# The last portion of the first modulation: from row products on TensorE to scaling on ScalarE and adding on GpSimd

## The chip, the cores and the metric

One core of one Trainium2 chip. The metric is the device time of one execution in microseconds (us); of several runs the median is compared.

## The reference, cut to what matters

The kernel computes one layer of a decoder for 256 tokens of width 1024. The change touches how the first modulation, a vector of 2 x 1024 numbers (shift and scale), comes out of the conditioning vector c:

```python
c_act = jax.nn.silu(c)                                  # c: (1, 1024)
mod = c_act @ w_ada[l] + b_ada[l]                       # w_ada: (1024, 6 * 1024)
sh1, sc1, g1, sh2, sc2, g2 = [m[:, None, :] for m in jnp.split(mod, 6, axis=-1)]
h = rms_norm(x, g_pre_mix[l]) * (1.0 + sc1) + sh1       # (1, 256, 1024)
y = hybrid_mixer(h, w_in[l], ...)                       # starts with h @ w_in
...
```

Everything is float32. Only sh1 and sc1, and of them only the last 256 of 1024 channels, are computed in another way after the change.

## The kernel before, in words

The kernel writes every engine's instructions out by hand, with semaphores between engines. The 1024 channels of h are KC = 8 chunks of 128, which lie on the partitions. The first ten output units (FIRST_UNIT = 10) of h @ w_in are computed chunk by chunk: for chunk k TensorE multiplies the chunk's columns of w_in by chunk k of h, and adds into eight PSUM banks. Each product takes three passes, since an operand is split into a rounded high part and the rest: ScalarE copies the raw weights into the high part (`chunk_cut_hi`, L862, or L886 for a whole chunk of 128x1224) and makes the high part of h (`chunk_h_hi`, L868); VectorE subtracts to get the low parts (L1243, L1289 and L1276). A chunk is 30 matmuls of 128x256 (all on L1641).

Chunk k of h can't be made before its shift and scale are there. These come in three portions, PORTION = [0, 3, 6, 8]: channels of chunks 0 to 2, 3 to 5, and 6 and 7. For each portion SyncE loads the columns of w_ada into the tile `ada`, four pairs of rows with a semaphore each (`load_ada`, L539). The tile holds for partition p the eight rows p*8 to p*8+7 of w_ada, so that `ada[:, k, a, :]` times `csil[:, k]` (silu(c), laid out in the same way) summed over k and over the partitions is the result. `row_products` (L1595) does that on TensorE: the weights are silu(c) repeated 32 times (`crep`), and `ada` streams past them, eight matmuls for two pairs, each in two records of the profile. ScalarE copies the row from PSUM to SBUF (`keep_row`, L856), TensorE turns it into columns (`turn_first` L1606, `turn_others` L1612), and VectorE adds bias and gain to give the columns `col` (`first_columns` L1250, `other_columns` L1259).

Where the row products stand in TensorE's order is a table: PRODUCTS_AT maps (chunk, number of matmuls of it that are done) to pairs, TURN_ROW_AT to the turn. Portion 2's products stand behind matmul 15 of chunk 4 and behind matmul 7 of chunk 5, its turn behind matmul 19 of chunk 5. Chunk 6 needs the columns. GpSimd builds masks in the first 4 us and has nothing to do from then until it loads further columns of w_ada for the second modulation (`load_part`, L672), once chunk 7 of h is made. `acc` is a tile of 128x2048 that holds squares of x at the start and those further sums later.

```python
            PRODUCTS_AT = {(1, 28): ((1, 0), (1, 1)), (2, 13): ((1, 2),), (2, 17): ((1, 3),), (4, 15): ((2, 0), (2, 1)), (5, 7): ((2, 2), (2, 3))}
            TURN_ROW_AT = {(2, 26): 1, (5, 19): 2}
```

Of the kernel before, what the change touches and what calls it, by code (L numbers as in the profile page):

```python
# [19 lines left out]
F32 = mybir.dt.float32  # L20
F32R = mybir.dt.float32r
ALU = mybir.AluOpType
ACT = mybir.ActivationFunctionType
AX_X = mybir.AxisListType.X

P = 128
D = 1024
KC = D // P
# [51 lines left out]
PORTION = [0, 3, 6, KC]  # L80
N_PORTIONS = len(PORTION) - 1
ADA_COLS = 3 * P
# [6 lines left out]
def columns_made(k):  # L89

    g = portion_of(k)
    return 4 * g + (2 if k == PORTION[g] else 4)
# [182 lines left out]
def decoder_layer(nc, x, c, w_ada, b_ada, g_pre_mix, g_post_mix, w_in, b_gate, w_proj_sb,  # L275
                  w_proj_moba, w_proj_dsa, w_o, g_pre_ffn, g_post_ffn, w_up, w_down, out):
    ctx = ExitStack()
    with ctx:
# [3 lines left out]
        def sem(name):  # L282
            return ctx.enter_context(nc.semaphore(name))
# [16 lines left out]
        csil = csil_all[:, 0:KC]  # L300
# [10 lines left out]
        ones = sb("ones", [P, P], F32R)  # L311
# [9 lines left out]
        acc = sb("acc", [P, 2 * D], scope=mix)  # L321
# [35 lines left out]
        gated_part.close()  # L357


        cut_part = ExitStack()  # L360
        sb("cut_pad", [P, TT * D + (3 * KC + N_OCH + FULL_OCH) * S + 2 * D + BANK + 4 * CAUSAL + 4 * P + 2 * TT * 8 + VEC_END],
           scope=cut_part)
# [3 lines left out]
        start = ExitStack()  # L366
        ada = sb("ada", [P, KC, 2, ADA_COLS], scope=start)
# [15 lines left out]
        bank = [psum[:, i, :] for i in range(8)]  # L383
# [5 lines left out]
        ada_in, mod_first, mod_cols = [sem(f"ada_in{p}") for p in range(KC // 2)], sem("mod_first"), sem("mod_cols")  # L389
# [2 lines left out]
        x_kept_act, x_kept_dve = sem("x_kept_act"), sem("x_kept_dve")  # L392
        x_raw_turned, root_ready, root_turned, rootrow_ready = (sem("x_raw_turned"), sem("root_ready"), sem("root_turned"),
                                                                sem("rootrow_ready"))
        row_kept, mod_turned, x_scaled, tmp_ready, chunk_hi, chunk_lo, chunk_done = (
            sem("row_kept"), sem("mod_turned"), sem("x_scaled"), sem("tmp_ready"), sem("chunk_hi"), sem("chunk_lo"), sem("chunk_done"))
        wo_in = [sem(f"wo_in{k}") for k in range(KC)]
# [14 lines left out]
        ss_ready, var_ready, sqrt_ready, xn_ready = sem("ss_ready"), sem("var_ready"), sem("sqrt_ready"), sem("xn_ready")  # L412
# [3 lines left out]
        ones_set, gate_in, gate_bias_in, gate_done, gate_hi, gate_lo, gate_ready = (  # L416
            sem("ones_set"), sem("gate_in"), sem("gate_bias_in"), sem("gate_done"), sem("gate_hi"), sem("gate_lo"), sem("gate_ready"))
# [7 lines left out]
        ln_ready, sp_ready, sp_masked, sp_hi, sp_lo, sums, a_ready, a_masked = (sem("ln_ready"), sem("sp_ready"), sem("sp_masked"), sem("sp_hi"), sem("sp_lo"),  # L425
                                                                 sem("sums"), sem("a_ready"), sem("a_masked"))
# [219 lines left out]
        def _(pool):  # L646
# [16 lines left out]
            def load_part(n):  # L663

                g, k, a = ADA_PARTS[n]
                if n < 2:
                    pool.wait_ge(tmp_ready, KC)
                    pool.wait_ge(chunk_hi, KC)
                else:
                    pool.wait_ge(acc_done, n - 1)  # L670
                c0 = D * (2 * g + a)
                pool.dma_start(ada_part[n % 2], ada_dram[:, k, c0:c0 + D]).then_inc(part_in[n % 2], 16)  # L672
# [6 lines left out]
            def load_gain(g):  # L679

                pool.wait_ge(gain_out[g], 16)
                pool.dma_start(gb[g][:, :], gain_dram[g:g + 1, :].to_broadcast([P, D])).then_inc(gain_in[g], 16)

            load_part(0)
            load_part(1)
            for u in range(FIRST_UNIT, N_UNITS):
# [6 lines left out]
                if u in SECOND_AT and SECOND_AT[u] in SB_NO:  # L693

                    i = SB_NO[SECOND_AT[u]]
                    n = SECOND_AT[u]
# [4 lines left out]
                if u in EXP_AT and EXP_AT[u] in SB_NO:  # L701

                    n = EXP_AT[u]
# [27 lines left out]
        def _(act):  # L731
# [102 lines left out]
            for w, k0 in ((b_ada, VEC_ADA), (g_pre_mix, VEC_PRE_MIX), (b_gate, VEC_GATE),  # L834
                          (g_post_mix, VEC_POST_MIX), (g_pre_ffn, VEC_PRE_FFN), (g_post_ffn, VEC_POST_FFN)):
                n = w.shape[0] * w.shape[1] // P
# [14 lines left out]
            def keep_row(g, c0, c1):  # L851

                act.wait_ge(gemv, (KC // 2) * (g + 1))
                if g:
                    act.wait_ge(mod_turned, g)
                act.activation(mrow[:, P * c0:P * c1], bank[5][:, P * c0:P * c1], ACT.Copy).then_inc(row_kept, 1)  # L856
# [7 lines left out]
            def chunk_h_hi(k):  # L864
# [3 lines left out]
                act.activation(hhi[:, k, :], h32[:, k, :], ACT.Identity, bias=col[0][:, k:k + 1],  # L868
                               scale=col[0][:, KC + k:KC + k + 1]).then_inc(chunk_hi, 1)

            for k in range(KC):
                if k in PORTION:
                    g = portion_of(k)
                    n = PORTION[g + 1] - k
                    keep_row(g, 0, 1)
                    if g:
                        keep_row(g, 1, n)
                    chunk_cut_hi(k, True)
                    chunk_h_hi(k)
                    chunk_cut_hi(k, False)  # L880
                    if g == 0:
                        keep_row(g, 1, n)
                else:
                    act.wait_ge(front_in[k], 16)
                    act.wait_ge(back_in[k], 16)
                    act.activation(chunk_view(whi, end_hi, k), chunk_view(raw, None, k), ACT.Copy).then_inc(w_hi, 2)  # L886
                    chunk_h_hi(k)
                if k == 2:
                    act.wait_ge(consts, 2)
                    act.activation(ones[:, :], neg1[:, :], ACT.Copy, scale=-1.0).then_inc(ones_set, 1)  # L890
                    act.activation(neg_all[:, :], neg1[:, :], ACT.Copy).then_inc(ones_set, 1)
                if k == KC - 1:
                    act.preload_act_table_set("natural_log_exp_and_others")
            for q in range(4):
# [4 lines left out]
            for u in range(FIRST_UNIT, N_UNITS):  # L899
# [4 lines left out]
                if u in EXP_AT and EXP_AT[u] in SB_NO:  # L904
                    n = EXP_AT[u]
# [12 lines left out]
                if u in NORM_AT and NORM_AT[u] in SB_NO:  # L918
                    n = NORM_AT[u]
# [9 lines left out]
                if u in EXP_AT and EXP_AT[u] in SOFT_NO:  # L929

                    n = EXP_AT[u]
# [8 lines left out]
                    for t, (c0, c1) in enumerate(((0, P), (P, CAUSAL))):  # L940
                        ins = act.activation(bufp[n % 2][:, c0:c1], bufa[n % 2][:, c0:c1], ACT.Exp,
                                             scale=SLOPES[2 * h + (branch == "ds")],
# [7 lines left out]
                if u in SECOND_AT:  # L950
                    n = SECOND_AT[u]
# [624 lines left out]
        def _(pe):  # L1576
# [31 lines left out]
            def turn_others(g):  # L1608

                pe.wait_ge(row_kept, 2 * g + 2)  # L1610
                for c in range(1, PORTION[g + 1] - PORTION[g]):
                    mm = pe.matmul(bank[6][:, 2 * c - 2:2 * c], mrow[:, P * c:P * (c + 1)], pick[:, :], start=True, stop=True)  # L1612
                mm.then_inc(mod_turned, 1)


            PRODUCTS_AT = {(1, 28): ((1, 0), (1, 1)), (2, 13): ((1, 2),), (2, 17): ((1, 3),), (4, 15): ((2, 0), (2, 1)), (5, 7): ((2, 2), (2, 3))}
            TURN_ROW_AT = {(2, 26): 1, (5, 19): 2}

            def warm_up(n):

# [159 lines left out]
            for t in range(TT):  # L1780
                mm = pe.transpose(bank[3][:, S + P * t:S + P * (t + 1)], rinv[:, t:t + 1].to_broadcast([P, P]), ident[:, :])
# [42 lines left out]
            def modulation_between(k, n):  # L1824

                for g, p in PRODUCTS_AT.get((k, n), ()):
                    row_products(g, p)
                if (k, n) in TURN_ROW_AT:
                    turn_first(TURN_ROW_AT[k, n])
                    turn_others(TURN_ROW_AT[k, n])  # L1830

            for k in range(KC - 1):
                if k in PORTION:
# [4 lines left out]
                for n, (i, u) in enumerate((i, u) for i in (0, 2, 1) for u in range(FIRST_UNIT)):  # L1838
# [4 lines left out]
                    mm = first_unit(u, k, (i,))  # L1843
# [4 lines left out]
            k = KC - 1  # L1848
# [37 lines left out]
            for f in range(KC):  # L1886
# [10 lines left out]
                for i, branch in enumerate(("sb", "mb", "ds")):  # L1897
                    dst = branches(f)[:, S * i:S * (i + 1)]
                    for c, ch in enumerate(BRANCH_CHUNKS[branch]):
                        if ch < FULL_OCH:  # L1900
                            mm = three(dst, [x[:, ch, :] for x in w], [ohi[:, ch, :], olo[:, ch, :]], c == 0, c == 2)
# [174 lines left out]
```

## Time and profile before

| what | value |
|---|---|
| median of 3 runs | 455.38 us (455.24 to 456.07) |
| profiled execution, time | 456.04 us |
| profiled execution, span | 454.3 us |
| busy share PE, DVE, ACT, POOL | 97%, 73%, 54%, 8% |
| share of PE in the chain that ended last | 94% |
| mean granted TensorE clock | 0.997 of full speed |

The span is that of one profiled execution, from its first to its last instruction; the time beside it is what the same execution took as a whole, 1.7 us more. PE is TensorE's matmuls, DVE is VectorE, ACT ScalarE, POOL GpSimd and SP SyncE; an L with a number is a line of the kernel, and times in the trace are in us from the start of the span.

### The profile page before, as it was taken

What the parts mean: (1) busy time and instruction counts of PE and PEld (TensorE: products, weight loads), DVE (VectorE), ACT (ScalarE), POOL (GpSimd) and SP (SyncE); (2) the same over time, 40 slices, a digit from 0 to 9 for tenths busy, and PEclk for the clock granted to TensorE, in tenths of its full rate; (3) what the DMA queues carried; (4) which work ended last, traced back from release to release, by engine and by line L of the source; (5) the groups of instructions that cost most, each with busy time, mean ns of one, the idle gap of its engine ahead of it and who ended that gap; (6) DMA issues with size and microseconds to landing.
All of it is one profiled execution on the core that took longest, in us unless ns stands there. A gap on an engine that the chain in (4) does not pass through costs nothing.

```text
span 454.3 us, 7880 instructions
## 1 busy us (share of the span) xinstructions
PE 439.9 (97%) x2966; PEld 388.9 (86%) x2966; DVE 330.7 (73%) x587; ACT 243.7 (54%) x432; POOL 34.8 (8%) x76
## 2 busy tenths in 40 slices
PE   4999999999999999999999999999999999999994
PEld 3678988999999899989997899888888888888883
DVE  4625668787998887956995785796696687678655
ACT  4424884556777656596553686533534525425332
POOL 2000102000322231000000001000000000000000
PEclk9999999999999999999999999999999999999998
DMA  8999466886788658746659526988648657530002
GB/s 288 383 378 345 153 231 222 280 297 236 241 302 291 188 180 283 235 150 202 195 200 365 186 68 184 378 302 277 228 159 269 218 190 272 185 138 0 1 0 92
DMA packets 61634, 99.86 MB, mean 220 GB/s; under 512 B 3892, under 2 KB 44452, under 8 KB 61604
## 3 DMA queue, kind: packets, MB, share of 16 engines
q1 hardware_dynamic: 56480, 81.57, 53.2%
q0 software_dynamic: 4960, 17.84, 11.5%
q8 instruction: 19, 0.31, 0.3%
q14 instruction: 11, 0.09, 0.1%
q10 hardware_dynamic: 164, 0.05, 0.0%
HBM read 98.40 MB, written 1.05 MB: 219 GB/s over the span
## 4 chain that ended last, share of the span: by engine, by line
PE 94%; DVE 2%; DMA 1%; issue 1%; ACT 1%; SPq 0%; DVEq 0%; ACTq 0%
PE psum L1579 17%; PE psum L1994 16%; PE psum L1580 16%; PE psum L1581 16%; PE psum L1995 8%; PE psum L1641 7%; PE psum L1941 3%; PE psum L1595 2%; PE psum L1768 1%; DVE wlo L1113 1%; DMA xt<-in_x_dram 1%; PE psum L1703 1%; PE psum L1701 1%; PE psum L1630 1%; PE psum L1750 1%
## 5 line engine op out<-in xcount | busy, mean ns | idle before, releaser
L1994 PE MATMUL psum<-hcut,whi 128*128 128x512 f32 x320 | 111.7, 392 | 0.0
L1995 PE MATMUL psum<-hcut,wlo 128*128 128x256 f32 x320 | 89.6, 280 | 0.0
L1579 PE MATMUL psum<-hcut,whi 128*128 128x256 f32 x280 | 82.1, 293 | 0.3 <-DVE wlo L1113 0.3
L1580 PE MATMUL psum<-hcut,whi 128*128 128x256 f32 x280 | 79.1, 283 | 0.0
L1581 PE MATMUL psum<-hcut,wlo 128*128 128x256 f32 x280 | 79.1, 282 | 0.0
L1113 DVE TENSOR_TENSOR wlo<-raw,whi 128x768 fp32r<-128x768 f32 (+3 forms) x68 | 64.4, 973 | 15.3 <-ACT whi L749 14.7
L1994 PEld LDWEIGHTS psum<-hcut,whi 128*128 128x128 f32 x320 | 59.9, 187 | 13.3
L1995 PEld LDWEIGHTS psum<-hcut,wlo 128*128 128x128 f32 x320 | 60.5, 189 | 0.3
L749 ACT ACTIVATE whi<-raw 128x768 fp32r<-128x768 f32 (+3 forms) x68 | 55.6, 850 | 6.8 <-PE psum L1905 3.2
L1579 PEld LDWEIGHTS psum<-hcut,whi 128*128 128x128 f32 x280 | 53.4, 191 | 5.5 <-ACT qk L829 2.0
L1580 PEld LDWEIGHTS psum<-hcut,whi 128*128 128x128 f32 x280 | 53.5, 191 | 0.0
L1581 PEld LDWEIGHTS psum<-hcut,wlo 128*128 128x128 f32 x280 | 53.5, 191 | 0.0
L1490 DVE TENSOR_TENSOR dlo<-draw,dhi 128x2048 fp32r<-128x2048 f32 x11 | 25.1, 2292 | 35.6 <-ACT dhi L1008 35.6
L1485 DVE TENSOR_TENSOR wlo<-raw,whi 128x1024 fp32r<-128x1024 f32 x36 | 42.4, 1220 | 3.0 <-ACT whi L1001 3.0
L1057 ACT ACTIVATE fsil<-fsil 128x256 f32<-128x256 f32 x20 | 8.4, 418 | 63.5 <-DVE fsil L1504 63.5
L1001 ACT ACTIVATE whi<-raw 128x1024 fp32r<-128x1024 f32 x36 | 35.9, 1045 | 0.0
L1580 PE MATMUL psum<-dlo,fhi 128*128 128x512 f32 x88 | 34.4, 391 | 0.0
L1579 PE MATMUL psum<-dhi,fhi 128*128 128x512 f32 x88 | 34.4, 391 | 0.0
L1581 PE MATMUL psum<-dhi,flo 128*128 128x512 f32 x88 | 34.2, 389 | 0.0
L1008 ACT ACTIVATE dhi<-draw 128x2048 fp32r<-128x2048 f32 x11 | 21.0, 1915 | 22.5 <-PE psum L1581 22.5
L1184 DVE SCALAR_TENSOR_TENSOR acc<-xn,csil,acc 128x1024 f32<-128x1024 f32 x21 | 26.9, 1282 | 4.6 <-DMA xn<-in_w_ada_dram 4.1
L1580 PE MATMUL psum<-wlo,hcut 128*128 128x320 f32 (+2 forms) x76 | 26.2, 345 | 0.0
(252 smaller groups left out, 817.3 us busy)
## 6 DMA issues: line engine op xcount, KB each, us to landing
raw<-in_w_up_dram SPq DMA_DIRECT2D x22, 1024.0 KB, 7.6
xn<-in_w_ada_dram POOLq DMA_DIRECT2D x32, 512.0 KB, 4.9
raw<-in_w_in_dram SPq DMA_DIRECT2D x6, 2048.0 KB, 9.0
draw<-in_w_down_dram SPq DMA_DIRECT2D x11, 1024.0 KB, 5.0
ada<-in_w_ada_dram SPq DMA_DIRECT2D x16, 384.0 KB, 9.2
raw<-in_w_in_dram SPq DMA_DIRECT2D x3, 1536.0 KB, 8.9
raw<-in_w_o_dram SPq DMA_DIRECT2D x8, 512.0 KB, 4.6
raw<-in_w_in_dram SPq DMA_DIRECT2D x3, 1280.0 KB, 7.0
```

The source lines that it names most:

```text
L749: act.activation(block_view(whi[b % 2], b)[0:p, chunks, cols], block_view(raw[b % 2], b)[0:p, chunks, cols], ACT.Copy).then_inc(w_hi, 1)
L1001: act.activation(block_view(whi[part], B_FFN)[:, 2 * q:2 * q + 2, :], block_view(raw[part], B_FFN)[:, 2 * q:2 * q + 2, :], ACT.Copy).then_ ...
L1113: dve.tensor_tensor(block_view(wlo[b % 2], b)[0:p, chunks, cols], block_view(raw[b % 2], b)[0:p, chunks, cols], block_view(whi[b % 2], b)[ ...
L1184: ins = dve.scalar_tensor_tensor(sums, part, csil[:, k:k + 1], sums, ALU.mult, ALU.add)
L1485: dve.tensor_tensor(block_view(wlo[part], B_FFN)[:, 2 * q:2 * q + 2, :], block_view(raw[part], B_FFN)[:, 2 * q:2 * q + 2, :], block_view(w ...
L1490: dve.tensor_tensor(dlo[slot][:, :, :], draw[slot][:, :, :], dhi[slot][:, :, :].bitcast(F32), ALU.subtract).then_inc(d_lo, 1)
L1579: pe.matmul(dst, a[0], b[0], start=first, stop=False)
L1580: pe.matmul(dst, a[0], b[1], start=False, stop=False)
L1581: return pe.matmul(dst, a[1], b[0], start=False, stop=last)
L1641: mm = pe.matmul(first_place(u)[0:n, :], w, h[:, k, :], start=k == 0 and i == 0 and u in (1, 2, 4, 6, 8), stop=k == KC - 1 and i == 2, ski ...
L1994: pe.matmul(dst[:, :], wh, hcut[:, k, :, :].rearrange("p a s -> p (a s)"), start=k == 0, stop=False)
L1995: mm = pe.matmul(dst[:, S:2 * S], wl, hhi[:, k, :], start=False, stop=k == KC - 1)
```

## The change

Portions 0 and 1 stay as they are. For portion 2, ScalarE multiplies `ada[:, k, :, 0:256]` in place by `csil[:, k]` for k = 0 to 7 (`scale_last`), two pairs behind chunk 4 and two behind chunk 5 (LAST_PAIRS_AT). GpSimd adds the eight up, into a part of `acc`: seven adds of 128x512, each waiting for the scaled operand and for the add before. TensorE then sums over the partitions with four matmuls (`last_columns`), whose weights are 128 columns of the sums and which stream one column of ones; they give columns at once, so the row copies and the turn are gone. They stand behind matmul 17 of chunk 5.

```diff
--- before.py
+++ after.py
@@ -357,6 +357,9 @@
         gated_part.close()
 
 
+        last_sums = acc[:, 0:2 * ADA_COLS].rearrange("p (a n) -> p a n", a=2)
+
+
         cut_part = ExitStack()
         sb("cut_pad", [P, TT * D + (3 * KC + N_OCH + FULL_OCH) * S + 2 * D + BANK + 4 * CAUSAL + 4 * P + 2 * TT * 8 + VEC_END],
            scope=cut_part)
@@ -392,6 +395,7 @@
         x_kept_act, x_kept_dve = sem("x_kept_act"), sem("x_kept_dve")
         x_raw_turned, root_ready, root_turned, rootrow_ready = (sem("x_raw_turned"), sem("root_ready"), sem("root_turned"),
                                                                 sem("rootrow_ready"))
+        last_scaled, last_added = sem("last_scaled"), sem("last_added")
         row_kept, mod_turned, x_scaled, tmp_ready, chunk_hi, chunk_lo, chunk_done = (
             sem("row_kept"), sem("mod_turned"), sem("x_scaled"), sem("tmp_ready"), sem("chunk_hi"), sem("chunk_lo"), sem("chunk_done"))
         wo_in = [sem(f"wo_in{k}") for k in range(KC)]
@@ -681,6 +685,17 @@
                 pool.wait_ge(gain_out[g], 16)
                 pool.dma_start(gb[g][:, :], gain_dram[g:g + 1, :].to_broadcast([P, D])).then_inc(gain_in[g], 16)
 
+
+            n_last = P * (PORTION[-1] - PORTION[-2])
+            sums = last_sums[:, :, 0:n_last]
+            for k in range(1, KC):
+                pool.wait_ge(last_scaled, k + 1)
+                if k == 1:
+                    pool.wait_ge(ss_ready, 4)
+                else:
+                    pool.wait_ge(last_added, k - 1)
+                pool.tensor_tensor(sums, ada[:, 0, :, 0:n_last] if k == 1 else sums, ada[:, k, :, 0:n_last], ALU.add).then_inc(last_added, 1)
+
             load_part(0)
             load_part(1)
             for u in range(FIRST_UNIT, N_UNITS):
@@ -868,12 +883,23 @@
                 act.activation(hhi[:, k, :], h32[:, k, :], ACT.Identity, bias=col[0][:, k:k + 1],
                                scale=col[0][:, KC + k:KC + k + 1]).then_inc(chunk_hi, 1)
 
+            def scale_last(p):
+
+                act.wait_ge(ada_in[p], 32 * N_PORTIONS)
+                for k in (2 * p, 2 * p + 1):
+                    part = ada[:, k, :, 0:P * (PORTION[-1] - PORTION[-2])]
+                    act.activation(part, part, ACT.Copy, scale=csil[:, k:k + 1]).then_inc(last_scaled, 1)
+
+
+            LAST_PAIRS_AT = {4: (0, 1), 5: (2, 3)}
+
             for k in range(KC):
                 if k in PORTION:
                     g = portion_of(k)
                     n = PORTION[g + 1] - k
-                    keep_row(g, 0, 1)
-                    if g:
+                    if g < N_PORTIONS - 1:
+                        keep_row(g, 0, 1)
+                    if 0 < g < N_PORTIONS - 1:
                         keep_row(g, 1, n)
                     chunk_cut_hi(k, True)
                     chunk_h_hi(k)
@@ -889,6 +915,8 @@
                     act.wait_ge(consts, 2)
                     act.activation(ones[:, :], neg1[:, :], ACT.Copy, scale=-1.0).then_inc(ones_set, 1)
                     act.activation(neg_all[:, :], neg1[:, :], ACT.Copy).then_inc(ones_set, 1)
+                for p in LAST_PAIRS_AT.get(k, ()):
+                    scale_last(p)
                 if k == KC - 1:
                     act.preload_act_table_set("natural_log_exp_and_others")
             for q in range(4):
@@ -1613,8 +1641,22 @@
                 mm.then_inc(mod_turned, 1)
 
 
-            PRODUCTS_AT = {(1, 28): ((1, 0), (1, 1)), (2, 13): ((1, 2),), (2, 17): ((1, 3),), (4, 15): ((2, 0), (2, 1)), (5, 7): ((2, 2), (2, 3))}
-            TURN_ROW_AT = {(2, 26): 1, (5, 19): 2}
+            PRODUCTS_AT = {(1, 28): ((1, 0), (1, 1)), (2, 13): ((1, 2),), (2, 17): ((1, 3),)}
+            TURN_ROW_AT = {(2, 26): 1}
+            LAST_COLUMNS_AT = (5, 17)
+
+            def last_columns():
+
+                pe.wait_ge(last_added, KC - 1)
+                pe.wait_ge(ones_set, 1)
+                pe.wait_ge(mod_cols, columns_made(PORTION[-2] - 1))
+                for c in range(PORTION[-1] - PORTION[-2]):
+                    for a in range(2):
+                        dst = bank[6][:, 2 * c - 2 + a:2 * c - 1 + a] if c else bank[7][:, a:a + 1]
+                        mm = pe.matmul(dst, last_sums[:, a, P * c:P * (c + 1)], ones[:, 0:1].bitcast(F32), start=True, stop=True)
+                    if c == 0:
+                        mm.then_inc(mod_first, 1)
+                mm.then_inc(mod_turned, 1)
 
             def warm_up(n):
 
@@ -1828,6 +1870,8 @@
                 if (k, n) in TURN_ROW_AT:
                     turn_first(TURN_ROW_AT[k, n])
                     turn_others(TURN_ROW_AT[k, n])
+                if (k, n) == LAST_COLUMNS_AT:
+                    last_columns()
 
             for k in range(KC - 1):
                 if k in PORTION:
```

In TensorE's order, around chunks 4 and 5 of the first ten units (hcut is h, whi and wlo the high and low parts of w_in), before:

```order
L1641 MATMUL psum<-hcut,wlo 128x256 x4
L1595 MATMUL psum<-ada,crep 32x256 x8
L1641 MATMUL psum<-hcut,wlo 128x256 x5
L1641 MATMUL psum<-hcut,whi 72x256
L1641 MATMUL psum<-hcut,whi 128x256 x9
L1641 MATMUL psum<-hcut,whi 72x256
L1641 MATMUL psum<-hcut,whi 128x256 x6
L1595 MATMUL psum<-ada,crep 32x256 x8
L1641 MATMUL psum<-hcut,whi 128x256 x3
L1641 MATMUL psum<-hcut,wlo 72x256
L1641 MATMUL psum<-hcut,wlo 128x256 x8
L1606 MATMUL psum<-pick,mrow 128x2
```

and after the change, up to the beginning of chunk 6:

```order
L1683 MATMUL psum<-hcut,wlo 128x256 x9
L1683 MATMUL psum<-hcut,whi 72x256
L1683 MATMUL psum<-hcut,whi 128x256 x9
L1683 MATMUL psum<-hcut,whi 72x256
L1683 MATMUL psum<-hcut,whi 128x256 x9
L1683 MATMUL psum<-hcut,wlo 72x256
L1683 MATMUL psum<-hcut,wlo 128x256 x6
L1656 MATMUL psum<-ones,acc 128x1 x4
L1683 MATMUL psum<-hcut,wlo 128x256 x3
L1683 MATMUL psum<-hcut,whi 72x256
L1683 MATMUL psum<-hcut,whi 128x256 x9
L1683 MATMUL psum<-hcut,end_hi 128x256
```

The sixteen row products are gone, and four matmuls of one column stand where the two turning ones stood, two places earlier.

In ScalarE's order, after the change, from chunk 4's cut to chunk 6's:

```order
L912 ACTIVATE whi<-raw 128x1224
L883 ACTIVATE hcut<-xn,col 128x256
L891 ACTIVATE ada<-ada,csil 128x2x256 x4
L912 ACTIVATE whi<-raw 128x1224
L883 ACTIVATE hcut<-xn,col 128x256
L891 ACTIVATE ada<-ada,csil 128x2x256 x4
L877 ACTIVATE end_hi<-raw 128x584
```

Before, the two L891 rows weren't there, and two copies `mrow<-psum 128x128` stood where the second one stands now: the first four scalings are now ahead of chunk 5's cut.

In GpSimd's order, after the change, from the masks to the first load:

```order
L664 AFFINE_SELECT dist<-dist 128x128 x2
L697 TENSOR_TENSOR acc<-ada 128x2x256
L697 TENSOR_TENSOR acc<-acc,ada 128x2x256 x6
L676 DMA xn<-in_w_ada_dram 128x1024 x3
```

The seven adds stand in what was one long wait.

## Rows read from the trace of the kernel before

**Rows 1.** The page, part 1: busy time, share of the span, instructions
```profile
PE 439.9 (97%) x2966; PEld 388.9 (86%) x2966; DVE 330.7 (73%) x587; ACT 243.7 (54%) x432; POOL 34.8 (8%) x76
```

**Rows 2.** Chain of waits, 30 to 56 us: start us, us, what
```profile
39.83 1.00 PE psum L1595 x16
...
43.63 1.00 PE psum L1595 x16
...
46.24 0.12 PE psum L1606 x2
46.35 0.22 PE psum L1612 x2
46.58 8.73 PE psum L1641 x71
```

**Rows 3.** Timeline of PE, start of chunk 6: start us, us, instruction
```profile
47.83 1.35 PE L1641 MATMUL psum<-hcut,end_hi 128*128 128x256 f32 x10
```

**Rows 4.** What waited on PE, whole span: us in total, times, longest us
```profile
PE psum L1579 <- DVE wlo L1113: 0.3, 1, 0.3
```

**Rows 5.** Timeline of ACT, 34 to 50 us
```profile
36.08 0.60 ACT L868 ACTIVATE hcut<-xn,col 128x256 fp32r<-128x256 f32 x1 [0.18 <-DVE col L1261]
36.59 1.22 ACT L886 ACTIVATE whi<-raw 128x1224 fp32r<-128x1224 f32 x1
37.71 0.58 ACT L868 ACTIVATE hcut<-xn,col 128x256 fp32r<-128x256 f32 x1
44.70 0.45 ACT L856 ACTIVATE mrow<-psum 128x128 f32<-128x128 f32 x2 [6.40 <-PE psum L1595]
```

**Rows 6.** Loads of ada, line L539, first pair of portion 2
```profile
L539 SPq DMA_DIRECT2D ada<-in_w_ada_dram x2: 378/448/517, 27.0 to 27.4; - x2
DMA to landing us min/median/max: 6.7/7.3/8.0
```

**Rows 7.** The same, its last pair
```profile
L539 SPq DMA_DIRECT2D ada<-in_w_ada_dram x2: 368/686/1003, 31.8 to 32.2; - x2
DMA to landing us min/median/max: 6.4/7.0/7.6
```

**Rows 8.** Groups by form, ACT: busy us, mean ns
```profile
L1033 ACT ACTIVATE xn<-xt,rinv 128x512 f32<-128x512 f32 x2 | 1.4, 715 | 0.8 <-DVEq L1137 0.8
```

**Rows 9.** Groups by form, POOL
```profile
L657 POOL CAST dist<-bufa 128x384 f32<-128x384 int32 x1 | 0.5, 502 | 0.0
...
L2064 POOL MEMSET const-float32-1.0<- 128x1 f32 x1 | 0.1, 98 | 0.0
```

**Rows 10.** Timeline of DVE, 36 to 50 us
```profile
38.42 1.43 DVE L1289 TENSOR_TENSOR wlo<-raw,whi 128x1224 fp32r<-128x1224 f32 x1
39.76 0.42 DVE L1276 TENSOR_TENSOR hcut<-bufp,hcut 128x256 fp32r<-128x256 f32 x1
```

**Rows 11.** Timeline of POOL, 0 to 62 us, and then 120 to 124 us
```profile
3.12 0.54 POOL L660 TENSOR_SCALAR_AFFINE_SELECT dist<-dist 128x128 f32<-128x128 f32 x2
...
120.55 2.50 POOL L707 TENSOR_SCALAR_AFFINE_SELECT bufp<-bufp 128x128 f32<-128x128 f32 x2 [2.10 <-DVE bufp L1357]
```

**Rows 12.** Timeline of DVE, 120 to 124 us
```profile
120.39 1.28 DVE L1184 SCALAR_TENSOR_TENSOR acc<-xn,csil,acc 128x1024 f32<-128x1024 f32 x1
121.58 2.54 DVE L1113 TENSOR_TENSOR wlo<-raw,whi 128x1024 fp32r<-128x1024 f32 x2
```

**Rows 13.** Windows at the end: stretch and length, busy by engine, PEclk, DMA
```profile
447.00:449.00 2.00, 1.17 (x6) 0.63 (x4) 0.75 (x2) 1.22 (x4) 0.00 (x0) 1.00 0.52 193
449.00:451.00 2.00, 0.00 (x0) 0.00 (x0) 1.89 (x6) 0.29 (x2) 0.00 (x0) 1.00 0.00 0
451.00:452.00 1.00, 0.00 (x0) 0.00 (x0) 0.84 (x2) 0.00 (x0) 0.00 (x0) 0.69 0.00 0
```

**Rows 14.** Chain of waits, first 13 us
```profile
9.92 1.35 PE psum L1595 x8
...
12.29 0.78 PE psum L1595 x8
```

## Prediction

> **What bounds the kernel now.** I read the busy shares first: TensorE is busy 97% of the span, GpSimd 8% [rows 1]. Then the chain of waits: from 30 to 56 us it is TensorE without a gap worth naming, and in it stand the two blocks of portion 2's row products, 1.00 us each, and the turn, 0.12 + 0.22 us [rows 2]. Then the list of waits: behind the start-up TensorE waits for another engine once, 0.3 us for VectorE near 124 us [rows 4]. So a microsecond that TensorE loses or wins between 40 and 50 us is lost or won in the total, but for some 0.3 us. The timelines of ScalarE and VectorE show what room they have there: ScalarE finishes chunk 5 of h at 38.3 us and then waits 6.40 us for the row of portion 2 [rows 5]; VectorE finishes chunk 5 at 40.2 us [rows 10]. GpSimd's masks end at 3.7 us [rows 11], and it has no work until 50 us.
>
> **TensorE, what goes and what comes.** Removed: 2 x 1.00 us of products and the turn, 0.12 + 0.22 = 0.34 us [rows 2]. Added: four matmuls with 128x128 float32 weights and one streamed column. The nearest rows are the two turning matmuls with the same weights and two columns, 0.34 us for the two [rows 2]; I take 0.8 us for four, with 0.68 as the low end and 0.9 as the high one (0.22 each for all). Net: 2.34 - 0.8 = **1.5 us less** if TensorE doesn't wait.
>
> **When TensorE comes to the new place.** Before, the turn stood behind matmul 19 of chunk 5 at 46.24 us [rows 2]. Without the products (-2.00) and two matmuls earlier (-0.25, from chunk 6's ten in 1.35 us with 0.12 from one to the next [rows 3]) TensorE is there at 44.0 us. If the sums are ready at time T, later than 44.0, the rest follows: 0.8 us for the columns and 13 matmuls of 0.114 us, 1.5 us (11 of them took 46.58 to 47.83 before [rows 2, 3]), and chunk 6 starts at T + 2.3. Before it started at 47.83. So **the change costs T - 45.5 us**, and T = 44.0 gives back the -1.5 above. Chunk 6 of h is not later than that: its first column needs half of the four matmuls (0.4), then VectorE and ScalarE as before, about 1.1 us, together T + 1.5.
>
> **ScalarE.** A scaling is 128x512 with a factor per partition; the same form took 0.715 us [rows 8], 0.62 from start to start when several follow (the cut of 1.22 us at 36.59 and the next at 37.71 show the 0.1 overlap [rows 5]). Its operands are there: the first pair of portion 2 lands at 27.4 + 8.0 = 35.4 us [rows 6], the last at 32.2 + 7.6 = 39.8 us [rows 7]. So four scalings run from 36.6 to 39.1, chunk 5's cut to 40.3, chunk 5 of h to 40.8, and four more from 40.7 to 43.3 us. Chunk 5 on TensorE starts near 41.5 (1.00 us earlier than before by the first products [rows 2]), so the delay of 2.5 us that chunk 5's cut gets has 0.7 us to spare. VectorE's subtraction for it moves from 38.4 to 40.3, ends 1.43 us later at 41.7 [rows 10], and its first use is ten matmuls behind 41.5, at 42.6. These parts cost nothing; that cover is thin, and half a microsecond more on ScalarE would show, but would be swallowed by the wait that comes next. The two row copies that go (0.45 us [rows 5]) free ScalarE where it was idle.
>
> **GpSimd, the term that decides.** The trace has no addition on GpSimd. Its nearest row with a streamed input is a cast of 128x384, 0.502 us; an instruction of one element takes 0.098 us [rows 9]. So one stream costs 0.404 us for 384 elements, 0.54 for 512. Low end for an add: one stream and the fixed part, 0.64 us. High end: the whole cast scaled up and doubled, 1.34 us. An add reads two tensors, and I take the streams one after the other: 0.10 + 2 x 0.54 = 1.17 us, and 0.1 us for the wait on its own semaphore, 1.27 from add to add. The Trainium skill, GPSIMD Engine Reference, section Performance versus the Vector engine, gives 4497 ns for a float32 add of 2048 elements; an estimate from that page is 1.1 to 1.2 us for 512, which would give the same sum within 0.3 us, where the single stream would give a kernel that is faster.
>
> The first add can start when two operands are scaled, at 38.0 us. Seven in a chain take 8.9 us: 46.9 us. The later operands (the last at 43.3) are never what an add waits for at this rate.
>
> On top comes VectorE. Two mask instructions of GpSimd took 2.50 us at 120.55, while VectorE ran a 1.28 us instruction with two tensor inputs and then subtractions of 1.2 us, where two of the same shape took 0.54 us on an idle chip [rows 11, 12]: each was held up for one VectorE instruction. In the adds' way stand chunk 5's subtraction, 1.43 us, and the 0.42 us one behind it [rows 10]. I count the large one, 1.4 us, with 0 and 1.85 as ends. The Trainium skill, SBUF — State Buffer, states that a VectorE instruction with two SBUF inputs and a GpSimd one that reads SBUF exclude each other for a whole instruction; by that page the full 1.4 stands, and the trace agrees in those rows.
>
> T = 38.0 + 8.9 + 1.4 = **48.3 us**: TensorE waits 4.3 us, and the cost is 48.3 - 45.5 = **+2.8 us**. Behind it all of VectorE's and ScalarE's work for chunks 6 and 7, and the load that waits for chunk 7's cut, moves with T; TensorE has 0.7 us more between T and chunk 6 than it had between the turn and chunk 6 (2.3 against 1.6), so none of them becomes a new wait. GpSimd's queue holds its first loads for the second modulation behind the adds; they wait for chunk 7 of h anyway, so the adds cost them nothing.
>
> The profiled execution took 456.04 us, 0.66 over the median of 455.38. I add to the median: 455.38 + 2.8 = 458.2 us. (In a profile: 456.04 + 2.8 = 458.8, a span of 457.1.)
>
> **The rivals.** *A, the forecast*: the adds take about 1.2 us each, blocked or not. Unblocked T is 46.9 and the cost +1.4, at the high ends +4; its own range is 456.7 to 459.4. For it speaks that an add has two streams and the cast one. Chance 0.48.
>
> *B, the clock falls*: TensorE would stand idle 4.3 us. At the end of the span its last matmul ends at 448.2, and the granted clock is 1.00 until 451 and 0.69 in the mean of the next microsecond [rows 13], so it fell from the 2.4 GHz level to that of 1.2 about 3.2 us behind the last matmul. At the start, eight products took 1.35 us, later 0.78 [rows 14], 1.7 times as long, and the slow ones came although TensorE had worked since 5 us. If the clock falls in the wait and 3 to 6 us of work run slowly, 1.3 to 2.6 us are added: 459.5 to 460.8. The Trainium skill, TensorE: Matmul & The Clock Gate, states the same of long idle gaps in the middle of a kernel. Against it: one drop in the trace says when it came once, not that every wait of 4 us brings it, and T may be earlier. Chance 0.22.
>
> *C, faster*: GpSimd streams both tensors at once, 0.64 + 0.1 us an add. Then ScalarE sets the end: its last product at 43.3, one add behind it, T = 44.1 and -1.4 us: 454.0. It decides from T under 44.6, which is an add-to-add time under 0.9 us if nothing blocks. For it: the mask instructions, which also read and write, are quick alone (0.27 us). Chance 0.14.
>
> *D, no difference*: an add-to-add time of 0.95 to 1.1 us without blocking, T 44.7 to 46.0, between -0.8 and +0.5: 454.6 to 455.9. Also the case in which VectorE's and TensorE's gains cancel. Chance 0.16.
>
> **How the numbers follow.** A measurement of this kernel can tell about 0.2%, 0.9 us, from no change. C is faster, with a little of D: 0.15. D without that, and A's lowest edge: 0.17. The rest of A and B: 0.68. The range reaches down to 454.2, which leaves out half of C, and up to 460.8, which leaves out the worst of B and of the price of an add: about 0.15 outside.
>
> **What would show it.** In the profile after: seven adds on GpSimd with 1.2 to 1.3 us from start to start and one gap or long one of some 1.4 us beside VectorE's 128x1224 subtraction; TensorE's four one-column matmuls starting near 48 us with a wait of 4 us for GpSimd ahead of them; chunk 6 near 50.6; scalings of 0.7 us on ScalarE with the last ending near 43.3. I am wrong if the adds come every 0.9 us or faster, if TensorE waits at chunk 5's start for ScalarE for more than a few tenths, or if what is lost at 48 us isn't in the total. A granted clock below 1.00 between 46 and 55 us would show B.

## The result, and the profile after

The changed kernel takes **461.3 us** in the median (460.59 to 462.72, 6 runs), the kernel before 455.44 us (455.13 to 456.27, 6 runs). The ratio is 1.0126, with a 95% interval of 1.0114 to 1.0137: 5.7 us slower. The forecast was 458.2 (+2.8 us) with a range of 454.2 to 460.8: the right side, half the size, and the measured time is outside the range. The profiled execution of the changed kernel took 460.59 us, with a span of 458.9.

The page of the kernel after, parts 1 and 2 (busy time; the granted clock in tenths by 40 slices of 11.5 us):

```profile
PE 439.4 (96%) x2938; PEld 390.6 (85%) x2938; DVE 333.4 (73%) x587; ACT 248.2 (54%) x438; POOL 44.2 (10%) x83
...
PEclk9999799999999999999999999999999999999998
```

Against [rows 1], TensorE has 28 instructions fewer and hardly less busy time, and GpSimd is busy 9.4 us more. New is the 7 in the fifth slice, 46 to 57 us. The wait that is new in that kernel's list of what TensorE waited for (us in total, times, longest; before: [rows 4]):

```profile
PE psum L1656 <- POOL acc L697: 5.3, 1, 5.3
```

The timeline of its POOL, 34 to 62 us, and a part of its chain of waits, 36 to 60 us (the chain now runs through GpSimd):

```profile
37.24 1.33 POOL L697 TENSOR_TENSOR acc<-ada 128x512 f32<-128x512 f32 x1 [33.58 <-ACT ada L891]
38.72 9.35 POOL L697 TENSOR_TENSOR acc<-acc,ada 128x512 f32<-128x512 f32 x6
```

```profile
40.16 2.31 POOL acc L697
...
42.60 1.27 POOL acc L697
...
46.81 1.27 POOL acc L697
...
48.13 1.86 PE psum L1656 x8
```

An add takes 1.27 us and the next starts 1.40 us after it; one took 2.31. The seventh ends at 48.08. The timelines of its ACT and DVE in the same place:

```profile
35.84 2.56 ACT L891 ACTIVATE ada<-ada,csil 128x512 f32<-128x512 f32 x4
38.31 1.21 ACT L912 ACTIVATE whi<-raw 128x1224 fp32r<-128x1224 f32 x1
39.43 0.58 ACT L883 ACTIVATE hcut<-xn,col 128x256 fp32r<-128x256 f32 x1
39.91 2.55 ACT L891 ACTIVATE ada<-ada,csil 128x512 f32<-128x512 f32 x4
```

```profile
37.34 1.39 DVE L1297 TENSOR_SCALAR bufp<-xn,col 128x256 f32<-128x256 f32 x1
39.62 1.68 DVE L1317 TENSOR_TENSOR wlo<-raw,whi 128x1224 fp32r<-128x1224 f32 x1 [0.90 <-ACT whi L912]
41.23 1.52 DVE L1304 TENSOR_TENSOR hcut<-bufp,hcut 128x256 fp32r<-128x256 f32 x1
```

ScalarE does what was forecast: four scalings in 2.56 us, the last ending at 42.46. This execution is 0.75 us ahead of the one before already at chunk 4 of h (35.33 against 36.08 in [rows 5]), so times of the two are compared after adding that; most of what follows is compared by lengths instead of by times. On VectorE, instructions of 0.4 us take 1.4 and 1.5 while GpSimd adds. Its PE, 38 to 62 us, and the windows around the wait (length, busy time of PE, PEld, DVE, ACT, POOL, granted clock, DMA share, GB/s):

```profile
41.84 0.98 PE L1683 MATMUL psum<-hcut,wlo 128*72 128x256 f32 x7
48.13 1.86 PE L1656 MATMUL psum<-ones,acc 128*128 128x1 f32 x8 [5.31 <-POOL acc L697]
49.85 0.99 PE L1683 MATMUL psum<-hcut,wlo 128*128 128x256 f32 x3
50.64 2.33 PE L1683 MATMUL psum<-hcut,whi 128*72 128x256 f32 x10
52.77 1.73 PE L1683 MATMUL psum<-hcut,end_hi 128*128 128x256 f32 x10
```

```profile
44.00:46.00 2.00, 0.00 (x0) 0.00 (x0) 0.00 (x0) 0.00 (x0) 1.85 (x2) 1.00 0.46 162
46.00:48.00 2.00, 0.00 (x0) 0.00 (x0) 0.00 (x0) 0.00 (x0) 1.86 (x2) 0.69 0.02 6
48.00:50.00 2.00, 1.87 (x9) 1.87 (x10) 0.79 (x4) 0.45 (x1) 0.07 (x1) 0.50 0.00 0
50.00:52.00 2.00, 2.00 (x10) 2.00 (x11) 1.97 (x6) 1.90 (x3) 0.00 (x0) 0.50 0.00 0
52.00:54.00 2.00, 2.00 (x13) 2.00 (x13) 1.96 (x4) 1.89 (x3) 0.68 (x1) 0.60 0.00 0
```

TensorE stands from 42.8 to 48.1 us with nothing to do. Within the wait the granted clock falls to 0.50, the level of 1.2 GHz, and is back at 2.4 GHz near 53.6: the eight records of the one-column matmuls take 1.86 us, ten matmuls of chunk 5 take 2.33 where ten took 1.35 in [rows 3]. From the end of the adds to chunk 6 it is 4.7 us, where 2.3 was forecast.

Where the 5.7 us arise can be read without the start-up: from the start of ScalarE's copy for chunk 4 of h (36.08 before, 35.33 after) to TensorE's first matmul behind the first ten units. That matmul is, before and after:

```profile
55.34 0.41 PE L1579 MATMUL psum<-whi,hcut 128*128 128x320 f32 x1
```

```profile
60.27 0.31 PE L1607 MATMUL psum<-whi,hcut 128*128 128x320 f32 x1
```

The stretch is 19.26 us long before and 24.94 after, 5.7 more. So what the change loses is lost there. The experiments below are read with the same stretch, each in its one profiled execution.

### The profile page after: what moved, and what is told of

It reads as the page before. It is cut to its first block, busy times and chain, and to the rows that moved or that the text cites. A ratio compares the mean times of both kernels' runs of the same rounds, so it can differ in the third digit from the quotient of the medians.

```text
span 458.9 us, 7842 instructions
## 1 busy us (share of the span) xinstructions
PE 439.4 (96%) x2938; PEld 390.6 (85%) x2938; DVE 333.4 (73%) x587; ACT 248.2 (54%) x438; POOL 44.2 (10%) x83
## 4 chain that ended last, share of the span: by engine, by line
PE 89%; DVE 3%; POOL 2%; DMA 2%; issue 1%; SPq 1%; ACT 1%; DVEq 0%; POOLq 0%; ACTq 0%
PE psum L1607 17%; PE psum L2038 16%; PE psum L1608 16%; PE psum L1609 16%; PE psum L2039 8%; PE psum L1683 5%; PE psum L1985 3%; POOL acc L697 2%; DMA ada<-in_w_ada_dram 2%; PE psum L1810 1%; DVE wlo L1141 1%; PE psum L1745 1%; PE psum L1743 1%; PE psum L1623 1%; SPq L543 1%
```

## The experiments

Two questions: how the 5.7 us divide between the wait and the clock, and whether GpSimd or ScalarE cost anything else on the way. Theory 1: a wait for seven slow adds, and a fallen clock on top. Its rivals differ by experiment. Ratios are to the kernel before in runs on the same chip, with their 95% interval; 1% is 4.56 us.

**The wait filled with transposes.** In `last_columns`, ahead of the wait:

```diff
+                for _ in range(40):
+                    pe.transpose(bank[5][:, 0:P], ident[:, :], ident[:, :])
```

> The changed kernel with 40 transposes of 128x128 into a PSUM bank that nobody reads, ahead of TensorE's wait for the sums: 40 x 0.125 = 5.0 us of work in a wait of 5.3 us. Theory 1 (the change costs a wait and, on top, a fallen clock): the granted clock stays at 1.00, the sums are ready at the same time (7 adds of 1.27 to 1.3 us, one of them held up), and the cost against the kernel before falls from 5.9 to about 3.2 us, ratio 1.007. Rival (all of the 5.9 us is the wait and what is late behind it; the clock costs nothing): 5.9 us, ratio 1.013.

Measured: ratio 1.0069 (1.0053 to 1.0085), +3.1 us, median 459.31. The mean granted clock was 0.997 or 0.998 in five of seven executions and 0.994 in two, where the changed kernel had 0.987 to 0.990 in all six of its own (the kernel before has 0.996 to 0.998; its clock falls only at the end of its span [rows 13]). The profiled execution is one of the two: a short fall, after the transposes. It is also the slowest of the seven, 462.66 us, but 2 us of that are start-up: its copy for chunk 4 of h starts at 38.13 us. The rival's 5.9 us is out: the clock costs 1.0126 - 1.0069, 2.6 us, and the wait alone 3.1. By the two intervals such a difference is uncertain by some 0.9 us.

**The same with ordinary matmuls.**

```diff
+                for _ in range(40):
+                    pe.matmul(bank[5][:, 0:S], whi[0][:, 0:P], hhi[:, 0, :], start=True, stop=True)
```

> As e1_busy_wait, with 40 matmuls of 128x256 of the kernel's usual type in place of the 40 transposes, 40 x 0.118 = 4.7 us. With transposes the mean granted clock was 0.997 in five executions and 0.994 in two. Theory 1: the clock stays, in all or nearly all executions, cost that of the wait alone, +3.1 to +3.5 us, ratio 1.007 to 1.008. If only uninterrupted work counted, the 0.6 us of wait that is left would still bring a fall in some: up to +5 us in those.

Measured: 1.0082 (1.0069 to 1.0095), +3.7 us, and a clock of 0.996 to 0.998 in all five executions. PE in its profile:

```profile
43.48 4.96 PE L1651 MATMUL psum<-hcut,whi 128*128 128x256 f32 x40
49.05 1.05 PE L1658 MATMUL psum<-ones,acc 128*128 128x1 f32 x8 [0.61 <-POOL acc L697]
...
51.58 1.36 PE L1685 MATMUL psum<-hcut,end_hi 128*128 128x256 f32 x10
```

At full clock the four column matmuls take 0.9 us (49.05 to 49.96, where the next starts), and chunk 6 starts 2.5 us after their start, where the forecast had 2.3. The wait costs 3.1 to 3.7 us, the clock 2.0 to 2.6. The traces divide it in the same way: the stretch from chunk 4 of h to the end of the first ten units takes 22.59 us here (36.13 to 58.72), 3.3 more than before, and 24.94 in the changed kernel, so the clock has 2.35 us of the 5.7.

**Three adds of seven.** GpSimd's loop stops after k = 3 and TensorE waits for three; four scaled products are left out of the sum.

```diff
-            for k in range(1, KC):
+            for k in range(1, 4):
...
-                pe.wait_ge(last_added, KC - 1)
+                pe.wait_ge(last_added, 3)
```

> The changed kernel with three adds of seven: the last four of the eight scaled products are not added (that part of the result is left out), the scalings stay. The third add ends near 42.5 us, when TensorE gets to its place. Theory 1: no wait, no fallen clock, so 2.34 us of products and turn are exchanged for about 0.8 us of four matmuls: 1.5 us faster than the kernel before, ratio 0.997. Rival (ScalarE's scalings make chunks 5 and 6 late, whatever the adds do): no gain, or slower, ratio 1.000 or more.

Measured: 0.9963 (0.9949 to 0.9977), 1.7 us **faster** than the kernel before. TensorE waits for nobody between 20 and 62 us. PE in its profile:

```profile
42.85 0.98 PE L1683 MATMUL psum<-hcut,wlo 128*72 128x256 f32 x7
43.68 0.95 PE L1656 MATMUL psum<-ones,acc 128*128 128x1 f32 x8
44.49 0.60 PE L1683 MATMUL psum<-hcut,wlo 128*128 128x256 f32 x3
```

So the exchange on TensorE is worth what was forecast, and ScalarE's eight scalings cost nothing. What makes the whole change slower is when the sum is ready, and the clock that falls meanwhile.

**Five adds of seven.** The same edit with 5; the last two products are left out.

> Five adds of seven (the last two products are not added, that part is left out). The fifth ends 2 x 1.4 us earlier than the seventh, near 45.3 us, and TensorE waits about 2.5 us instead of 5.3. Theory 1 with a clock that falls only in a long wait: the clock stays at 1.00 and the cost is the changed kernel's without the clock, less 2.8: 3.2 - 2.8 = +0.4 us, ratio 1.001. Rival (the clock falls in this wait too): +2.5 to +3 us, ratio 1.006.

Measured: 1.0030 (1.0016 to 1.0043), +1.4 us, a wait of 2.63 us in the profile. Of twelve executions ten took 456.64 to 457.77 us, and two, with a mean granted clock of 0.990 where the ten have 0.993 or more, took 458.97 and 459.10. So the full fall comes in some executions and not in others, and it costs some 1.9 us where it comes. The rest isn't all at full clock either: seven of the ten have 0.993 to 0.995, under the lowest of the kernel before on this chip (0.996), which would be a short fall; the other three, the profiled one among them, have 0.996 or more. The +0.4 expected came out a microsecond higher. In the profiled execution the stretch from chunk 4 of h to the end of the first ten units is 19.81 us, +0.55, close to what was expected, and from chunk 4 of h to the end of the span it is +1.15 us. What comes on top is in part a wait near 66 us, which the kernel before doesn't have:

```profile
PE psum L1607 <- DVE wlo L1141: 0.6, 1, 0.6
```

ScalarE, and VectorE behind it, had waited there for a load of weights, 2.5 us and not 1.0 as before.

**The matmuls later.** `LAST_COLUMNS_AT = (5, 29)` in place of `(5, 17)`.

> The changed kernel with the four matmuls behind matmul 29 of chunk 5, not 17, so that 12 matmuls (1.4 us) run in the wait, which shrinks from 5.3 to about 3.9 us. Chunk 6 is then held by its first column instead, ready about 1.5 us after the sums, not by the 2.3 us of columns and matmuls: 0.8 us less. Theory 1, with a clock that falls in most executions also in a wait of 3.9 us: +5.7 - 0.8 to 1.2, so +4.5 to +4.9 us, ratio 1.010 to 1.011, and a mean granted clock of 0.990. If the shorter wait keeps the clock: +2.3 us, ratio 1.005, and 0.997. Rival (what hangs on chunk 6 of h is not what sets the end): +5.7 us as before.

Measured: 1.0111 (1.0096 to 1.0125), +5.1 us, and a clock of 0.988 to 0.994. The wait is 3.91 us, the fall as in the changed kernel: windows of its profile:

```profile
46.00:48.00 2.00, 0.00 (x0) 0.00 (x0) 0.00 (x0) 0.00 (x0) 1.82 (x2) 0.78 0.00 0
48.00:50.00 2.00, 1.98 (x9) 1.98 (x9) 0.89 (x4) 0.54 (x2) 0.00 (x0) 0.50 0.00 0
50.00:52.00 2.00, 2.00 (x10) 1.91 (x11) 1.93 (x7) 1.82 (x4) 0.00 (x0) 0.50 0.00 0
```

That is 0.7 us less than the changed kernel's 5.7, at the edge of what was expected. But the two intervals overlap, so the medians don't exclude the rival, that the place is worth nothing. The stretch in the two profiles differs by 1.1 us (23.81 against 24.94), which speaks for the place.

**Later, and the wait filled.** The place (5, 29) with 28 unused matmuls.

> The changed kernel with both: the four matmuls behind matmul 29, and 28 unused matmuls of 128x256 (3.3 us) ahead of the wait. Theory 1: the two effects add up. The clock keeps its level (0.996 to 0.998; it fell in all executions of e4_late_place), and chunk 6 is held by its first column, 1.5 us behind the sums and not 2.3: cost e5_matmul_busy's 0.8% less 0.8 us, so +2.7 us, ratio 1.006. Rival (the later place is worth nothing): +3.7 us, 1.008.

Measured: 1.0078 (1.0064 to 1.0091), +3.6 us: the rival's number, not Theory 1's, which counted on the clock. The clock fell here in four executions of five (0.992; 0.997 in the fifth). PE in its profile:

```profile
44.58 3.50 PE L1651 MATMUL psum<-hcut,whi 128*128 128x256 f32 x28
48.73 1.05 PE L1658 MATMUL psum<-ones,acc 128*128 128x1 f32 x8 [0.65 <-POOL acc L697]
...
50.40 2.06 PE L1685 MATMUL psum<-hcut,end_hi 128*128 128x256 f32 x10 [0.40 <-ACT hcut L883]
```

Chunk 6 starts 1.67 us after the column matmuls do, 0.86 less than with the place at 17 (2.53, above): the later place does its part. But the ten matmuls of chunk 6 take 2.06 us in place of 1.36, since the granted clock is 0.63 in the mean of 50 to 54 us. Ahead of that TensorE had two waits, of 0.65 and 0.40 us, and between them matmuls of one column. That is where the 0.86 us went in this trace: chunks 6 and 7 take 8.80 us (50.40 to 59.20), and 7.14 with the ordinary matmuls at 17 and the clock whole (51.58 to 58.72), 1.7 us more. In the totals it shows less: the fifth execution, with the clock whole, took 459.29 us and the others 459.27 to 459.89. So the later place starts chunk 6 earlier, and no run here shows a gain in the total from it with the clock kept up.

**The adds beside the kernel before.** Row products and turn stay; GpSimd does seven adds on the raw rows, which nobody uses. (TensorE waits for them before chunk 7, where they are long done.)

```diff
+            for k in range(1, KC):
+                pool.wait_ge(ada_in[k // 2], 32 * N_PORTIONS)
...
+                pool.tensor_tensor(sums, ada[:, 0, :, 0:n_last] if k == 1 else sums, ada[:, k, :, 0:n_last], ALU.add).then_inc(last_added, 1)
```

> The kernel before, row products and turn as they were, with the seven adds on GpSimd put beside them, on the raw loaded rows, and their result unused. It tells what the adds do to the others by themselves. Theory 1: some of VectorE's instructions for chunk 5 are held up by about 1 us each, for which there is room; TensorE doesn't wait: 0.0 to +0.3 us, ratio 1.000. Rival (a good part of the 3.1 us that the changed kernel loses without the clock is VectorE being blocked by GpSimd): +1 us or more, ratio 1.002 and up.

Measured: 1.0028 (1.0017 to 1.0040), +1.3 us: the rival's number. DVE and PE in its profile:

```profile
35.60 1.28 DVE L1273 TENSOR_TENSOR col<-col,vecs 128x2 f32<-128x2 f32 x1
36.81 0.15 DVE L1274 TENSOR_TENSOR col<-psum,vecs 128x2 f32<-128x2 f32 x1
36.99 1.53 DVE L1282 TENSOR_SCALAR bufp<-xn,col 128x256 f32<-128x256 f32 x1
38.44 1.42 DVE L1302 TENSOR_TENSOR wlo<-raw,whi 128x1224 fp32r<-128x1224 f32 x1
39.78 1.50 DVE L1289 TENSOR_TENSOR hcut<-bufp,hcut 128x256 fp32r<-128x256 f32 x1
```

```profile
39.91 0.81 PE L1654 MATMUL psum<-hcut,wlo 128*72 128x256 f32 x5 [0.80 <-DVE wlo L1302]
```

A VectorE instruction on two columns takes 1.28 us, from 35.60 to 36.88, and the first add runs from 35.58 to 36.87. The next, with one input in PSUM, takes 0.15 us, but it starts at 36.81 and has hardly an add beside it: the second starts at 37.08. By themselves the adds block VectorE and through it TensorE, which waits 0.80 us. They start at 35.6 here, as soon as the first rows have landed, and not at 37.2, behind two scalings, and so are in the way of chunk 4; in the changed kernel the blocked instructions are chunk 5's, and TensorE waits for none of them there.

**Sharing the sum out.** VectorE multiplies and adds rows 0 to 2, 3 and 7, ScalarE scales 4 to 6, GpSimd adds those with two adds, VectorE adds that; columns at (5, 24).

```diff
+                    ins = dve.scalar_tensor_tensor(sums, ada[:, k, :, 0:n], csil[:, k:k + 1], sums, ALU.mult, ALU.add)
...
+                if k == 4:
+                    for n in (0, 1, 2):
+                        add_last(n)
+                if k == 5:
+                    for n in (3, 7):
+                        add_last(n)
+                    add_pool_sum()
```

> A version that shares the sum out: VectorE multiplies and adds rows 0 to 2 in one instruction each behind chunk 4, and 3 and 7 behind chunk 5, ScalarE scales 4, 5 and 6, GpSimd adds those three up with two adds, VectorE adds GpSimd's sum; the four matmuls stand behind matmul 24 of chunk 5. Estimated from the rows (0.67 us for a VectorE instruction of 128x512, half of 1.28 for 1024): sums ready near 44 us, no wait of TensorE over 0.5 us, clock at 1.00: 1.0 to 1.8 us faster than the kernel before, ratio 0.996 to 0.998. If VectorE's chunk 5 is held up by GpSimd and makes TensorE wait for the low parts, no gain, ratio 1.000.

Measured: 1.0043 (1.0029 to 1.0057), 2.0 us **slower** than the kernel before, all of the estimate missed. DVE in its profile:

```profile
40.16 1.40 DVE L1294 TENSOR_SCALAR bufp<-xn,col 128x256 f32<-128x256 f32 x1
...
42.81 1.51 DVE L1301 TENSOR_TENSOR hcut<-bufp,hcut 128x256 fp32r<-128x256 f32 x1
44.24 1.60 DVE L1312 SCALAR_TENSOR_TENSOR acc<-ada,csil,acc 128x512 f32<-128x512 f32 x2
45.95 0.69 DVE L1321 TENSOR_TENSOR acc<-acc,ada 128x512 f32<-128x512 f32 x1
```

The two adds hold VectorE up by 1.0 and 1.1 us, in front of the sums, which are ready at 46.6 and not 44. TensorE waits 1.64 us, and the clock falls all the same (0.994 or 0.995 in seven of eight executions). In the totals the cost of that fall doesn't show: the eighth, at 0.999, took 458.80 us, the others 457.00 to 458.51. In the profiled execution it does: chunks 6 and 7 take 8.65 us (48.41 to 57.06) in place of 7.14, so 1.5 us of the 1.8 that its stretch is longer than before.

**No GpSimd at all, half of the rows.** On the kernel before, VectorE multiplies and adds rows 0 to 3 behind chunk 4, TensorE takes them in with two products by ones, pairs 2 and 3 and the turn stay.

```diff
+                for a in range(2):
+                    mm = pe.matmul(bank[5][32 * a:32 * a + 32, 0:n], ones[:, 0:32].bitcast(F32), last_sums[:, a, 0:n],
+                                   start=True, stop=False, tile_position=(0, 32 * a))
...
+                if k == 4:
+                    for n in range(4):
+                        add_last(n)
```

> The kernel before, where VectorE alone multiplies and adds rows 0 to 3 of the last portion behind chunk 4 (four instructions, 0.6 to 0.8 us each, about 3 us, done near 41 us), and TensorE sums them with two row products by ones in place of eight; pairs 2 and 3 and the turn stay as they were. No GpSimd, no ScalarE. TensorE saves 1.00 us and pays 0.25: 0.75 us faster if it waits for nothing, ratio 0.998. If VectorE's low part of chunk 5, now ready near 42.7 us, comes late, the gain is gone and up to 0.5 us more, ratio 1.001.

> v2_four_rows once more, since its interval (0.9974 to 1.0002) just touches 1. If the 0.9 us that chunk 6 starts earlier in its trace lasts to the end in most executions, the ratio is 0.998 to 0.999 again; if the wait for the last pieces of the branch projections' weights near 222 us (1.1 us in its trace, none in the kernel before) gives it back as a rule, it is 1.000.

Measured: 0.9988 (0.9974 to 1.0002), and again 0.9985 (0.9974 to 0.9996): 0.5 and 0.7 us faster, little, and clear of 1 only in the second set (455.14 us against 455.72); still, it is the one version here that computes the whole result and isn't slower than the kernel before. In both its profiles TensorE now waits near 222 us; from the list of waits of the second:

```profile
PE psum L1597 <- ACT whi L752: 1.0, 1, 1.0
```

behind a transfer of projection weights, which in the profile of the kernel before let ScalarE wait 2.6 us but TensorE not at all. So TensorE, earlier by 0.8 us at the end of the first ten units, runs into a load there. In the two profiles that takes all of the gain: from chunk 4 of h to the end of the span they take 418.4 us, the profile of the kernel before 418.2. What the medians gain is then not in these two executions. All this is read from traces, not tried by moving the load.

## Why the prediction was wrong, point by point

**What bounds.** Right. TensorE had no slack, and what it lost near 48 us is in the total.

**TensorE's exchange**, 1.5 us less: right, 1.7 measured with three adds. The row products were worth somewhat more than their 2.00 us: chunk 4 to the turn took 8.2 us before, of which 49 matmuls of 0.118 are 5.8, so 2.4 belong to the products.

**When TensorE comes to the place.** Too late by 0.45 us, for the same reason: 44.0 forecast, 42.8 + 0.75 = 43.55 measured.

**ScalarE at nothing.** Right; 0.715 us a scaling was forecast and four took 2.56 us.

**An add, 1.17 + 0.1 us.** 1.27 + 0.13 measured, and 1.04 us of blocking in place of 1.4. From first start to last end 10.84 us, 10.3 forecast: seven adds took 0.9 us more than the forecast gave them and the blocking 0.4 less, so it is partly luck that T is this close. So T is 48.1 + 0.75 = 48.85, 48.3 forecast, and the formula T - 45.5 gives +3.35: the two experiments with the clock kept up measured 3.1 and 3.7, the forecast had 2.8. Had the clock stayed, the measured time would have been within 1 us of the forecast.

**The step that failed is B, "the clock falls", chance 0.22.** The sum adds the wait to the median, 455.38 + 2.8, with nothing for the clock in a wait of 4.3 us. The fall was priced at 1.3 to 2.6 us and costs 2.0 to 2.6; the chance was wrong. It came in each of the six executions. The argument against it was that one drop at the end of a span doesn't say every wait of 4 us brings it. But the sum itself had a wait of 4.3 us, longer than the 3.2 us after which the clock fell in [rows 13], and the wait came out at 5.3; with that row the fall belonged in the forecast, not beside it: 458.2 + 2 to 2.6 = 460.2 to 460.8, and with the half microsecond by which T came later than forecast, 461. The Trainium skill, TensorE: Matmul & The Clock Gate, section Why this matters for your kernels, warns of idle gaps in the middle of a kernel; the trace agrees, 0.50 in the windows from 48 us.

One reading behind B's price was wrong. The prediction took the slow products at the start (1.35 us against 0.78, 1.7 times [rows 14]) for the lower clock. The windows of that profile give 1.00 for all of that stretch:

```profile
5.00:11.00 6.00, 5.15 (x25) 3.52 (x25) 4.08 (x14) 3.67 (x7) 0.00 (x0) 1.00 1.04 376
```

Why those products were slow is open. What the lower level does can be read from the changed kernel against the one with ordinary matmuls in its wait: ten matmuls of chunk 5 take 2.13 us from first start to the next start, and 1.17 at full clock, 1.8 times as long. That B's price fits all the same is luck in part.

**Blocking.** Counted in one direction only, VectorE holding up GpSimd. The other direction was left out, and it costs 1.0 to 1.1 us for each short VectorE instruction met (1.39 in place of 0.41, 1.52 in place of 0.42). In the changed kernel it happens to be hidden.

## What to carry to other kernels

When work moves off a saturated TensorE, the question is not whether the other engine has time, but when its chain of dependent steps ends: here seven adds of 1.40 us against 5.6 us until TensorE needs them. A forecast wait on TensorE is to be priced with its clock: when the same trace shows the clock falling behind an idle stretch no longer than the wait, the fall belongs in the sum, here 2.0 to 2.6 us on 3.1 to 3.7. A shorter wait is no proof against it, as three experiments show. And work for GpSimd beside VectorE is no free work: put the same adds beside the unchanged kernel first, and see what they cost.

## What was not expected of the hardware

- GpSimd's adds hold up a VectorE instruction with one tensor input too: the 128x256 TENSOR_SCALAR took 1.37 to 1.53 us beside adds, 0.41 without. An addition on two columns took 1.28 us in place of 0.16. Whether an instruction with an input in PSUM is held up too isn't shown. The Trainium skill, SBUF — State Buffer, section Who interferes with whom, lists `tensor_scalar` among the instructions that can take the shared pair of ports; the trace agrees with that.
- The length of the longest wait does not tell by itself whether the clock falls. By the mean clock it fell in all ten executions with a wait of 5.3 or 3.9 us. With 2.63 us it fell fully in two of twelve and, it seems, for a short time in seven more, but not in the profiled one. With 1.64 us it fell for a short time in seven of eight, and in four of five with waits of 0.65 and 0.40 us around the one-column matmuls; with 0.61 us alone it fell in none of five. (Each length is that of the one profiled execution.) Transposes in the wait kept it up in five of seven executions, ordinary matmuls in five of five. What sets it beyond that is open.
